# A new order of work on TensorE: forget gate and query first, the other projections between narrower score products

## The reference

```
u = rmsnorm(tok) @ w_in                       # 7 groups of 512 columns: bg, cg, hv, q, fx, iv, og
bx = bg * hv;  y_conv = cg * conv3(bx)        # causal, width 3
f = lb + (1 - lb) * sigmoid(fx);  kk = 1 - f;  b = cumsum(log f)
scores[t, s] = sum_k q[t,k] kk[s,k] exp(b[t,k] - b[s,k])     for s <= t, per head
o = scores @ iv + (q * exp(b)) @ S0
S = exp(b_last) * S0 + (kk * exp(b_last - b))^T @ iv
y_rec = headnorm(o) * gain * silu(og)
h = tok + [y_conv, y_rec] @ w_out
out = h + moe(rmsnorm(h))                     # 32 experts, top 4, each 1024 -> 2048 -> 1024
```

## Time and profile before

| what | value |
|---|---|
| median of 3 runs | 1161.4 us (1159.9 to 1164.58) |
| the profiled execution's own time | 1161.72 us |
| its span in the profile | 1160.0 us |
| TensorE busy | 1062.0 us, 92% |
| VectorE / ScalarE / GpSimd busy | 287.3 / 168.3 / 48.6 us |
| read from memory | 427.5 MB |
| mean granted TensorE clock | 0.987 of full |

### The profile page before, as it was taken

The page is one execution under the profiler, slowest core; times in us unless marked ns, Lnnn a source line. Parts: engine busy times, 40 slices in busy tenths (PEclk is TensorE's granted clock), DMA queues, the critical chain, the costliest instruction groups (busy, mean ns, idle before and its releaser), DMA issues.

```text
span 1160.0 us, 13518 instructions
## 1 busy us (share of the span) xinstructions
PE 1062.0 (92%) x5617; PEld 485.9 (42%) x5617; DVE 287.3 (25%) x513; ACT 168.3 (15%) x381; POOL 48.6 (4%) x71
## 2 busy tenths in 40 slices
PE   6998899899999999899989998999898989898986
PEld 5666764443434343434343434343434343434322
DVE  3447742630202020202020202020202020202023
ACT  3311103310101010101010101010101010101012
POOL 3260012000000000000000000000000000000000
PEclk9999999899999999999999999999999999999998
DMA  9860238399999999999999999999999999999991
GB/s 335 292 241 4 99 147 314 112 409 429 428 425 429 427 429 427 428 430 426 431 427 427 431 426 431 427 428 430 426 431 427 429 429 427 431 425 429 427 429 76
DMA packets 47842, 431.46 MB, mean 372 GB/s; under 512 B 4942, under 2 KB 13686, under 8 KB 23136
## 3 DMA queue, kind: packets, MB, share of 16 engines
q1 hardware_dynamic: 45760, 428.23, 88.4%
q0 software_dynamic: 752, 2.56, 0.7%
q10 hardware_dynamic: 1296, 0.20, 0.1%
HBM read 427.50 MB, written 3.48 MB: 372 GB/s over the span
## 4 chain that ended last, share of the span: by engine, by line
PE 61%; DMA 32%; DVE 3%; ACT 2%; issue 2%; SPq 1%; ACTq 0%; DVEq 0%
DMA ring<-in_expert_w 31%; PE ps L1635 19%; PE ps L1590 17%; PE ps L1286 7%; PE ps L1531 5%; PE ps L1268 2%; PE ps L1397 2%; PE ps L1548 2%; ACT mem L722 2%; PE ps L1624 2%; PE ps L1342 1%; DMA ring<-in_meta_tokens 0%; SPq L387 0%; PE ps L1260 0%; PE ps L1276 0%
## 5 line engine op out<-in xcount | busy, mean ns | idle before, releaser
L1590 PE MATMUL ps<-ring,mem 128*64 128x512 f32 x2048 | 459.2, 596 | 42.4 <-DMA ring<-in_expert_w 41.9
L1590 PEld LDWEIGHTS ps<-ring,mem 128*64 128x64 f32 x2048 | 155.1, 137 | 335.8 <-issue 334.8
L1635 PE MATMUL ps<-ring,mem 128*64 128x512 f32 x1024 | 225.2, 597 | 5.3 <-ACT mem L738 3.0
L1117 DVE TENSOR_TENSOR mem<-mem,ps 128x1024 f32<-128x1024 f32 x32 | 39.1, 1222 | 463.6 <-PE ps L1548 463.6
L1635 PEld LDWEIGHTS ps<-ring,mem 128*64 128x64 f32 x1024 | 86.0, 138 | 133.6 <-issue 133.6
L731 ACT ACTIVATE mem<-mem 128x512 f32<-128x512 f32 x32 | 20.2, 630 | 569.0 <-DVE mem L1179 569.0
L1286 PE MATMUL ps<-mem,ring 128*128 128x280 f32 x320 | 82.7, 417 | 1.0 <-DVE mem L933 0.6
L1548 PE MATMUL ps<-mem 128*128 128x512 f32 (+3 forms) x192 | 80.0, 610 | 0.0
L1286 PEld LDWEIGHTS ps<-mem,ring 128*128 128x128 f32 x320 | 62.6, 200 | 18.7 <-issue 2.8
L1531 PEld LDWEIGHTS ps<-mem 128*128 128x128 bf16 x1080 | 60.3, 98 | 12.2 <-issue 12.2
L1531 PE MATMUL ps<-mem 128*128 128x128 bf16 x1080 | 62.9, 219 | 0.0
(11 more groups left out here) (268 smaller groups left out, 521.0 us busy)
## 6 DMA issues: line engine op xcount, KB each, us to landing
ring<-in_expert_w SPq DMA_DIRECT2D x192, 2048.0 KB, 26.8
ring<-in_w_in SPq DMA_DIRECT2D x7, 2048.0 KB, 20.6
ring<-in_w_out SPq DMA_DIRECT2D x2, 2048.0 KB, 10.1
ring<-in_state_rec SPq DMA_DIRECT2D x4, 512.0 KB, 10.5
out<-ring SPq DMA_DIRECT2D x4, 512.0 KB, 11.0
out<-mem SPq DMA_DIRECT2D x5, 256.0 KB, 5.2
ring<-in_x_prompt SPq DMA_DIRECT2D x2, 512.0 KB, 4.4
mem<-in_x_prompt POOLq DMA_DIRECT2D x2, 512.0 KB, 4.1
```

The lines of the kernel that those rows point to most:

```text
L1117: dve.tensor_tensor(h3[:, m], h3[:, m], ps[:, 4 + 2 * m:6 + 2 * m, :].rearrange("p a n -> p (a n)"), ALU.add)\
L1590: done = mm(ps[CAP * e:CAP * e + CAP, b, :], xgT4[:, k, t, CAP * e:CAP * e + CAP], ring[:, slot[e], col:col + HALF], start=False, stop=(t ...
L1635: done = mm(ps[CAP * e:CAP * e + CAP, 4 + half, :], actT3[:, 4 * v + t, CAP * e:CAP * e + CAP], ring[:, slot[e], col:col + HALF], start=(v ...
```

## The change

It has four parts. SP loads the query weights ahead of the value weights, and TensorE projects FX, then QG. The value and output gate rows join the list `SCHEDULE`, each 128-token product cut into two halves of four steps; the list is written out by hand, with the gates ("gate") and the query decay ("qhat") as pieces of it. Output gate rows use banks 5, 6 and 7, where BG, HV and CG come later, so their first products wait for the gates (`sog_sb`). And a level's score product has only the 64 later (query) columns as its moving side, and the predicated copy takes 256 elements instead of 512.

```diff
+        def level(n):
+            return [("score", n + 1 + n // LEVELS)]
+
+        DIAG = [[("score", 0)], [("score", LEVELS + 1)]]
+        SCHEDULE = [("rows", (IV, 0, 0))] + DIAG[0] + [("rows", (IV, 0, 1))] + level(0)
+        SCHEDULE += [("rows", (IV, 1, 0)), ("khat", 0)] + level(1) + [("rows", (IV, 1, 1))] + level(2)
+        SCHEDULE += [("rows", (IV, 2, 0))] + level(3) + [("rows", (OG, 0, 0))] + level(4)
+        SCHEDULE += [("rows", (OG, 0, 1))] + level(5) + [("rows", (OG, 1, 0))] + level(6)
+        SCHEDULE += [("gate", 0), ("rows", (OG, 1, 1))] + DIAG[1] + [("rows", (OG, 2, 0))] + level(7)
+        SCHEDULE += [("gate", 1), ("gate", 2), ("proj", (BG, 0)), ("outer", 0), ("proj", (HV, 0))] + level(8)
+        SCHEDULE += [("proj", (BG, 1)), ("outer", 1), ("proj", (HV, 1))] + level(9)
+        SCHEDULE += [("proj", (BG, 2)), ("outer", 2), ("qhat", 0), ("proj", (HV, 2))] + level(10) + [("state", 0)]
+        SCHEDULE += [("proj", (BG, 3))] + level(11) + [("recur", 0), ("proj", (HV, 3))] + level(12)
+        SCHEDULE += [("proj", (CG, 0))] + level(13) + [("proj", (CG, 1)), ("os", 0), ("proj", (CG, 2))]
+        SCHEDULE += [("recur", 1), ("proj", (CG, 3))]
...
             sp.dma_start(w_sb[FX], w_group(FX)).then_inc(win_in[FX], 16)
+            sp.dma_start(w_sb[QG], w_group(QG)).then_inc(win_in[QG], 16)
             sp.dma_start(w_sb[IV], w_group(IV)).then_inc(win_in[IV], 16)
-            sp.dma_start(w_sb[QG], w_group(QG)).then_inc(win_in[QG], 16)
...
             for what, a in SCHEDULE:
+                if what == "rows" and a[0] == IV and (a[2] or a[1] == 2):
+                    i = a[1]
+                    act.wait_ge(iv_ps, i + 1)
+                    act.activation(vtok3[:, i, 0:WIDE[i]], ps[:, 5 + i, 0:WIDE[i]], ACT.Copy).then_inc(v_sb, 1)
...
+                if what == "gate":
+                    g = sog3[:, a] if a < 2 else sogS
+                    dve.wait_ge(og_exp, a + 1)
+                    link(dve.tensor_scalar(g, g, 1.0, None, ALU.add))
+                    link(dve.reciprocal(g, g))
+                    dve.tensor_tensor(g, g, ps[:, 5 + a, 0:WIDE[a]], ALU.mult).then_inc(sog_sb, 1)
...
                     else:
-                        m = blocks3[:, STEPS[n][1]].bitcast(U32)
-                        ins = dve.copy_predicated(into, bcast(m.unsqueeze(1), [P, HEADS, P]), got)
+                        i = 1 << STEPS[n][1]
+                        got = ps[:, 2 + a % 2, 0:256].rearrange("p (h m i) -> p h m i", h=HEADS, i=i)
+                        later = sc3[:, c].rearrange("p (h m a i) -> p h m a i", h=HEADS, a=2, i=i)[:, :, :, 1]
+                        m = blocks3[:, STEPS[n][1]].bitcast(U32).rearrange("p (m a i) -> p m a i", a=2, i=i)[:, :, 1]
+                        ins = dve.copy_predicated(later, bcast(m.unsqueeze(1), list(later.shape)), got)
...
             for h in range(HEADS):
                 if h >= 2:
                     pe.wait_ge(q_sb, h - 1)
                 columns_of(QG, h, h % 2, q_ps)
...
+                if what == "rows":
+                    g, i, half = a
+                    if half == 0:
+                        pe.wait_ge(win_in[g], 16)
+                        if g == OG:
+                            pe.wait_ge(v_sb, i + 1)
...
                     if j:
                         pe.wait_ge(used, j)
+                    else:
+                        pe.wait_ge(sog_sb, bank - 4)
...
+                        left = wl3[:, n % 2]
+                        later = cut(left, 2 << STEPS[n][1])[:, :, 1 << STEPS[n][1]:]
...
+                            m = later.shape[1] // HEADS
+                            last = mm(ps[:, 2 + a % 2, h * 64:(h + 1) * 64], left[:, at],
+                                      later[:, h * m:(h + 1) * m], start=True, stop=True)
```

More of the change, by code:

```diff
@@ L628, in _ @@
                 act.activation(qS3[:, h], ps[:, h % 2, 0:32], ACT.Copy).then_inc(q_sb, 1)
[L630 to L635, removed]
-            for what, a in SCHEDULE:
+            for what, a in SCHEDULE:
+                if what == "rows" and a[0] == IV and (a[2] or a[1] == 2):
+                    i = a[1]
+                    act.wait_ge(iv_ps, i + 1)
+                    act.activation(vtok3[:, i, 0:WIDE[i]], ps[:, 5 + i, 0:WIDE[i]], ACT.Copy).then_inc(v_sb, 1)
+                if what == "rows" and a[0] == OG and (a[2] or a[1] == 2):
+                    i = a[1]
+                    act.wait_ge(og_ps, i + 1)
+                    if i == 2:
+                        act.wait_ge(sums_sb, 1)
+                    act.activation(sog3[:, i] if i < 2 else sogS, ps[:, 5 + i, 0:WIDE[i]], ACT.Exp, scale=-1.0)\
+                        .then_inc(og_exp, 1)
                 if what == "proj" and a[0] == BG:
@@ L905, in _ @@
             weigh(0)
             for what, a in SCHEDULE:
+                if what == "gate":
[4 more added lines that the diff above has]
+                    dve.tensor_tensor(g, g, ps[:, 5 + a, 0:WIDE[a]], ALU.mult).then_inc(sog_sb, 1)
+                if what == "qhat":
+                    dve.wait_ge(v_sb, 3)
+                    dve.tensor_tensor(cut(v_heads, P), bcast(vtok3[:, 2, 0:P].unsqueeze(1), [P, HEADS, P]),
+                                      bcast(head.unsqueeze(2), [P, HEADS, P]), ALU.mult)
+                    for c in range(2):
+                        dve.wait_ge(decay_exp, c + 2)
+                        link(dve.tensor_copy(decay_all[:, 4 * c:4 * c + 4],
+                                             qhat3[:, c].rearrange("p (h t) -> p h t", h=HEADS)[:, :, P - 1]))
+                        dve.tensor_tensor(qhat3[:, c], qhat3[:, c], qC3[:, c], ALU.mult).then_inc(qhat_sb, 1)
@@ L1262, in _, with rows_of @@
                         last.then_inc(xT_ps, 1)
-            def rows_of(g, i, bank, done):
+            def rows_of(g, i, half, bank, done):
                 at = TILE_COL[i]
-                for t in range(KT):
+                for t in range(4 * half, 4 * half + 4):
                     last = mm(ps[:, bank, :], xT3[:, t, at:at + P], w_sb[g][:, t, :],
                               start=(t == 0), stop=(t == KT - 1))
-                last.then_inc(done, 1)
+                if half:
+                    last.then_inc(done, 1)
             def stacked(g, bank, done):
@@ L1301, in _ @@
                 columns_of(QG, h, h % 2, q_ps)
[L1303 to L1309, removed]
-            for what, a in SCHEDULE:
+            for what, a in SCHEDULE:
+                if what == "rows":
[4 more added lines that the diff above has]
+                            pe.wait_ge(v_sb, i + 1)
+                    done = iv_ps if g == IV else og_ps
+                    if i < 2:
+                        rows_of(g, i, half, 5 + i, done)
+                    else:
+                        stacked(g, 7, done)
                 if what == "proj":
```

35 lines of the change are left out of this document (8 added, 27 removed).

## The result

| | before | after |
|---|---|---|
| median of 20 runs each | 1161.23 us (1157.63 to 1164.58) | 1162.97 us (1161.39 to 1164.77) |
| profiled execution: own time / span | 1161.72 / 1160.0 us | 1164.77 / 1163.0 us |
| output product starts | 168.60 us | 172.37 us |
| experts start | 223.94 us | 227.19 us |

The ratio is 1.0016, 95% interval [1.0008, 1.0023]: 1.7 us slower by medians, where 1159.5 us, 0.2% faster, was forecast. Both lie within half a percent of the kernel before, and the range held the time. But the interval leaves out 1, so the sign is measured, and it is the other one. The profiled execution of the kernel after is the slowest of its 20, 1.8 us above their median, and that of the kernel before lies 0.5 us above its own; so the two profiles differ by 3.0 us where the medians differ by 1.7.

What follows compares the result with a forecast made beforehand. The end was taken to follow TensorE's start on the experts, whose weights fill the DMA engines. Losses 3.9 + 2.5 + 4.3 + 2.5 + 0.8 = 14.0 us against 13.9, scores saving 2.3: 1159.5 us, range 1150.5 to 1167.

Steps and rivals of the forecast that it cites:

- What bounds the kernel: Expert weight transfers fill the DMA engines; the end follows TensorE's start on the experts, microsecond for microsecond.
- The rival without effect at the end: Expert weight stream starts no earlier, so the gain doesn't reach the end: 1161.7 us, chance 0.07.
- The query copy: Query column 2 waits for ScalarE's copy behind level 1's exponentials: TensorE stands 41.4 to 45.3 us, 3.9 us lost.
- The clock behind it: Low TensorE clock after the query copy wait: 2.5 us lost, bounds 0 and 3.5.
- Rows between scores: Projection rows in halves between scores give VectorE time for the weights, so 8.2 us of score waits go.
- the 0.8 us of idle time: TensorE's idle time before the output product beyond the 8.2 us of score waits, kept as a loss in the new order.
- the sum: Losses of 14.0 us against 13.9, scores give 2.3: output product 2.2 us earlier, 1159.5 us.
- The gates: Gates amid the scores: HV 0 waits for gate 1, held up by GpSimd's work, 4.3 us, bounds 0.3 and 10.3.
- gate 1 is held up at each instruction: Slower rival: GpSimd gets in between each two VectorE instructions, HV 0 waits 10.3 us, 1165.5 us; chance 0.15.
- the output product past 168.6 us: One of two alternative signs for the slower rival, the other being stalls in the levels under GpSimd's first five products.
- Score products of 64 columns: Score matmuls of 14 levels at 0.09 us instead of 0.111: 2.3 us saved, bounds 0 and 4.0.
- Clock behind the gate: Low TensorE clock after HV 0's wait for gate 1: 2.5 us lost.

Runs made afterwards that it cites:

- the split late: Changed kernel with GpSimd's expert bias split moved behind the list, under the output product: 1151.10 us, ratio 0.9910.
- the fills: Changed kernel with the bias split's five reading GpSimd instructions replaced by fills of about the same duration, leaving expert biases out: 1152.98 us, ratio 0.9929.
- the old list with query first: Kernel before with only the query's load, columns and copies moved ahead of the value's: 1175.22 us, ratio 1.0118.
- both edits: Changed kernel with the bias split behind the list and ScalarE's copies of query columns 0 and 1 around the decay exponential: 1143.86 us, ratio 0.9855.

## Why the prediction was wrong

**What bounds the kernel: right.** The end followed the start of the experts, and that followed the output product: 3.8, 3.3 and 3.0 us later at the output product, the experts and the span's end. The rival without effect at the end is out.

**The query copy: right, to the step.** The prediction had TensorE standing from 41.4 to 45.3 us, 3.9 us. It stood 3.90 us, until ScalarE had finished the exponentials of level 1 and the copy. TensorE's timeline after, with the idle time before in brackets:

```profile
45.12 10.65 PE L1296 MATMUL ps<-mem,ring 128*128 128x280 f32 x32 [3.90 <-ACT mem L631]
```

And what ScalarE did first, in its timeline:

```profile
43.35 1.37 ACT L622 ACTIVATE ring<-ring 128x256 f32<-128x256 f32 x4
44.62 0.36 ACT L629 ACTIVATE mem<-ps 128x256 f32<-128x256 f32 x1
```

The clock behind it cost 10.65 - 7.64 = 3.0 us, where 2.5 were taken (bounds 0 to 3.5). This price is no constant: behind the same wait of 3.9 us the two columns took 9.22 us with the split late, 9.37 with the fills and 9.44 in the old list with query first, a loss of 1.6 to 1.8 us.

**Rows between scores: right.** The waits for weights are gone, and of the 0.8 us of idle time kept in the sum 0.2 are left after, beside the wait under the gate, and 0.5 in the version with both edits.

**The gates: the step that failed.** "HV 0 waits 4.3 us" was the sum's value between the bounds 0.3 and 10.3; it measured 9.67, in TensorE's timeline after:

```profile
111.77 5.99 PE L1296 MATMUL ps<-mem,ring 128*128 128x280 f32 x16 [9.67 <-DVE mem L903]
```

The place was right, and the mechanism too: GpSimd's split holds VectorE up under gate 1. Its size was not. The prediction let GpSimd's first long product hold the difference, and one cast the gate's addition, and had VectorE go through freely between. The traces show turns at each instruction, which is the rival "gate 1 is held up at each instruction", given 0.15: difference behind the long product (99.3 us), a weighting behind each of two casts (103.4), the addition behind the second long product (107.6). The rival's steps are these, each 1.0 to 1.7 us later than written. I had read the two meetings in the trace before as proof that VectorE stands until GpSimd is done. But both are single instructions; they could not say what happens to a queue of instructions on each engine. From a row that shows one meeting the sum should have gone to the upper bound wherever VectorE has several instructions with SBUF operands one behind another, since nothing in the trace showed that VectorE gets two in a row.

That the steps come later has a cause that the prediction left out: GpSimd is held up too. Its five products met the levels before. GpSimd's row, and VectorE's weightings beside it:

```profile
78.18 8.71 POOL L516 TENSOR_TENSOR ring<-ring,mem 128x1024 f32<-128x1024 f32 x4
78.69 4.15 DVE L882 TENSOR_TENSOR ring<-ring,mem 128x256 f32<-128x256 f32 x2
```

The four products took 8.71 us instead of 7.45. They started 0.5 us later than the sum has them, so the split's long product started at 94.73 us instead of 92.9. VectorE's two weightings took 4.15 us instead of 0.75 here too. TensorE didn't wait, since the levels had time in hand, as the prediction has it; the output product past 168.6 us was the sign of the slower rival that did show.

The Trainium skill, "SBUF — State Buffer", section "Who interferes with whom", says that a VectorE instruction with two SBUF inputs contends with a GpSimd instruction that reads SBUF, not with one that only writes it, and that of two contending instructions the first has the shared ports for its whole duration. The trace agrees with both: 4.02 us for the difference under a reading subtraction, 0.68 us under fills. When both engines had contending instructions waiting, it was the other engine's turn each time.

The clock behind this wait cost 5.99 - 3.79 = 2.2 us (2.5 taken). So the failed step is the wait put down for GpSimd's split: 4.3 us in the sum, 9.67 measured, because VectorE was held up at each contending instruction and not twice.

**Score products of 64 columns: wrong.** 0.09 us a matmul were taken, from rows with 32 and 8 columns, a saving of 2.3 us. They run at 0.84 / 8 = 0.105 us, and what that saves the next product gives back (4.33 us from score to score, narrow or wide). The saving is nil, the lower bound. The Trainium skill's rule, "TensorE: Matmul & The Clock Gate", section "LDWEIGHTS (loading the stationary operand)", which the prediction set aside, would have given 0.107 us a matmul and 0.45 us in all. That is the nearer figure: with 128 x 128 weights, 0.105 us agrees with it. The rows that I preferred were misread. The transposes of 8 columns have weights of 8 x 128 only. The four products of 32 columns have 128 x 128 weights, but only three loads of weights fall between the two starts that I took; the first had begun at 203.7 us, under the product before. In the timeline of TensorE's weight loads before, the three take 0.11 us each:

```profile
204.11 0.33 PEld L1451 LDWEIGHTS ps<-mem 128*128 128x128 f32 x3 [0.24 <-issue]
```

**The sum.** The output product was predicted at 166.4 us. Wait 9.67 instead of 4.3: +5.4. Scores: +2.3. Start of the value products 55.61 instead of 55.5: +0.1. Clock behind the gate: -0.3. Idle time beside the waits, 0.2 instead of 0.8: -0.6. The products alone took 104.9 us where TensorE had no large gap (the window of both edits), and 105.6 were counted: -0.7. Together 172.6 us; measured 172.37. The 0.2 us that remain are not assigned to a cause.

So one term, the wait under the gate, turned a small gain into a loss; with it right alone the output product would have been put at 171.8 us and the sign would have been right. The scores alone, at their measured worth of nothing, would have made the forecast 168.7 us, no change. That the measured time lies inside the range all the same is owed to the rival with the long wait, for which the range had room, and not to the sum.

**What the change could have been.** Both causes are a matter of order on an engine off the chain. With the bias split behind the list and two copies ahead of the exponentials the same change makes the kernel 1.5% faster than before.

## What to carry to other kernels

When a reordering moves the moment at which another engine's background work starts, place that work anew under the new order, instruction by instruction; if GpSimd then reads SBUF beside a queue of short VectorE instructions, count a whole GpSimd instruction ahead of each of them, until a trace shows otherwise. When TensorE will have to wait for an engine that walks a list, look at what stands ahead of the awaited instruction in that list: two copies moved up were worth 6 us. And judge a shortened matmul by the distance between the starts on both sides of it, never by its own row.

## What the runs showed of the hardware

- VectorE and GpSimd took turns where GpSimd's instructions read SBUF and VectorE's were differences, weightings or additions of a number: 4.02, 4.13 (two) and 3.76 us for VectorE instructions of 0.68, 0.75 (two) and 0.45 us. GpSimd paid as well, with 8.71 us for four products of 7.45. A copy of four elements took 4.02 us instead of 0.16.
- A reciprocal of 512 elements took 3.35 us beside GpSimd's reads as without them, and a product with one input in PSUM kept its 0.69 us (at 76.64 us before, under the subtraction from 75.05).
- Fills on GpSimd left VectorE's differences and weightings alone (0.68 and 0.76 us) and stretched its addition of a number to 1.16 us.
- Behind a gap of 3.9 us the granted clock over the next 10.7 us was 0.73, a loss of 3.0 us; behind one of 9.67 us it was 0.76 over 8.3 us, a loss of 2.2 us. The longer gap did not cost more, and gaps of 3.9 us in three other kernels cost 1.6 to 1.8 us. Clocks between half and full are means over a stretch at either of the two levels, 1.2 and 2.4 GHz.
- Products of 64 columns on 128 x 128 float32 weights follow one another at 0.105 us, those of 128 columns at 0.111, and in a list without large gaps both give the same time (105.44 and 105.53 us for the stretch).
